# First attention without the scaling by the inverse row sum; the head norm takes epsilon times the squared sum

## The chip, the cores and the metric

The kernel runs on one core of one Trainium2 chip. The metric is the device time of one execution in microseconds (us), as a median over runs. Engines are named as the profile names them: PE (TensorE, matmuls), PEld (its weight loads), DVE (VectorE), ACT (ScalarE), POOL (GpSimd) and SP (SyncE, which issues most transfers). "L1688" is line 1688 of the kernel before.

## The reference

The kernel computes a two-layer encoder over 1024 tokens of width 1024 in float32. Layer 0 is a differential attention, layer 1 a latent attention, and a squared-ReLU MLP follows each. Only the attention of layer 0 is touched. It has 8 heads; each head has two score maps, and for a block of 128 queries:

```python
s = einsum(q, k) * scale + rel_bias            # two components c = 0, 1
p = softmax(masked s)                          # each component by itself
a = p[:, :, 0] - lam * p[:, :, 1]
o = a @ v                                      # 128 values for one query
o = o * rsqrt(mean(o * o) + 1e-6) * w * (1 - lam_init)
```

With e1 and e2 the exponentials and l1 and l2 their row sums, a = e1/l1 - lam * e2/l2. That is (e1 - lam * (l1/l2) * e2) / l1. The division by l1 is one factor for each query, and the norm that follows takes it out again, except for the epsilon in it.

## The kernel before, in words

A head is worked off in eight steps, s = 0 to 7, one for each block of 128 queries; step s has (s+1)*128 keys. All engines run the same order of steps, written out by hand (`heads0`, one for each engine), and meet at semaphores. Two query blocks make a pair, and the output and its norm are computed by pairs (256 queries).

For one block s the work goes round the engines so:

- PE computes both score maps (`scores0`, L1682), one step ahead: in step s it issues those of block s+1.
- DVE adds the bias, takes the maximum and writes the sum to `prob(s)` (`max0`, L1157), and writes the negated maxima (L1161).
- ACT takes both exponentials with their row sums l1, l2 in `st[:, 6:8]` (`exps0`, L712).
- DVE takes the reciprocals of both sums (L1210), the factor -lam*l1/l2 (L1212), and then e1 plus factor times e2 over the whole width (L1214), which raises `a_raw`.
- ACT multiplies the result by 1/l1 in place (`scale0`, L718) and raises `a_ready`.
- In step s+1 PE waits for `a_ready` and transposes the block in 128x128 pieces into PSUM tile TB (`turn0`, L1585), in one or two groups of up to four; ACT and DVE take it out of TB as a high and a low part (L696, L1137), and DVE raises `t_evac`. TB is a single bank, so a group waits until the one before is taken out.
- When both blocks of a pair are there, PE multiplies them with V (`values0`, L1666) into VB: in step 2 for pair 0, in 4 for pair 1, in 6 for pair 2, and in step 0 of the next head for pair 3.

The norm of a pair follows one step later, in steps 3, 5 and 7, and in step 1 of the next head for pair 3. ACT squares VB (`out_square`, L740), PE sums the squares over the partitions with a product by `ones` (`square_sum`, L1688), ACT takes the logarithm with scale and epsilon and then exp(-0.5 x) (`rms_of_pair`, L727 and L730), and DVE multiplies (`norm_out`, L1190). In ACT's order `scale0` of the step stands between `out_square` and `rms_of_pair`. After `rms_of_pair` ACT rounds a slab of weights for the next head (`split_hi`, L650) in steps 0, 1 and 3, and DVE computes its low part (`split_lo`, L1055).

PE has more in its order: the projections of the next head, in twelve half pieces of 12 products (`proj0`, L1578, `HALF_PIECES`). There is one after the transposes of a block in every step but step 0, and a second one after `square_sum` or the scores in steps 1, 2, 3, 5 and 7 as listed. ACT and DVE take the finished pieces out (`copy_piece0`, L690; `lo_piece0`, L1176, both between the exponentials and the second group of transposes of a block). The last head has no projections. DVE also does 8 multiply-adds of another product in each head (`ada_mac`, L1069); PE sums their result with 4 products that stream one column each (`mod_block`, L1599).

Of the kernel before, what the change touches and what calls it, by code (L numbers as in the profile page):

```python
# [18 lines left out]
ALU = mybir.AluOpType  # L19
ACT = mybir.ActivationFunctionType  # L20

P = 128
# [5 lines left out]
NQ = S // P  # L28
# [4 lines left out]
HD = 64  # L33
# [6 lines left out]
LN_EPS, RMS_EPS = 1e-5, 1e-6  # L40
# [7 lines left out]
PAIR = 2 * P  # L48
# [71 lines left out]
def encoder(nc, x, c, pos_offset, ada_w, ada_b, ln_g, ln_b, rel_table, w_qkv, w_o0, lq1, lk1, lq2,  # L120
# [3 lines left out]
    with ctx:  # L124
        def sb(name, shape, dt=F32):
            return ctx.enter_context(nc.sbuf_tensor(name, shape, dt))
# [18 lines left out]
        ones = sb("ones", [P, P])  # L145
# [4 lines left out]
        aff = sb("aff", [P, 7, KT])  # L150
        st = sb("st", [P, 18])
        soft = sb("soft", [P, 4 + 2 * NQ])
        posi = sb("posi", [P, 1], I32)
        lam = sb("lam", [P, 4 + REL_BUCKETS])

        ident = cst[:, 0:P]
# [14 lines left out]
        def prob(s): return X[:, 2 * (s % 2), :], X[:, 2 * (s % 2) + 1, :]  # L171
        bias = [X[:, 4, :], X[:, 5, :]]
        vT = X[:, 6, :]
        osq, oraw, orstd, ofin = (X[:, 7, i * PAIR:(i + 1) * PAIR] for i in range(4))
# [21 lines left out]
        VB = ps("VB", HALF)  # L196
# [8 lines left out]
        eps_ln, eps_rms = st[:, 11:12], st[:, 12:13]  # L205
# [437 lines left out]
        def _(act):  # L643
# [68 lines left out]
                    nc.scalar.activation(w, w, ACT.Exp, bias=st[:, 4 + comp:5 + comp],  # L712
                                         accum_out=st[:, 6 + comp:7 + comp]).then_inc(a0["p_ready"], 1)

            def scale0(h, s):
                act.wait_ge(a0["a_raw"], NQ * h + s + 1)
                w = prob(s)[0][:, 0:(s + 1) * P]
                nc.scalar.activation(w, w, ACT.Copy, scale=st[:, 8:9]).then_inc(a0["a_ready"], 1)  # L718

            def a_hi(h, s, part):  # L720
                dst, nb = at_group(0, s, part, AT0)
                copy_t(a0, 14 * h + group_of0(s, part), dst, t_psum(nb))
# [1 line left out]
            def rms_of_pair(h, pair):  # L724

                act.wait_ge(a0["ms_ready"], 4 * h + pair + 1)
                nc.scalar.activation(orstd, VB[:, PAIR:2 * PAIR], ACT.Ln, scale=1.0 / (2 * HD), bias=eps_rms)\  # L727
                    .then_inc(act_seq, 1)
                act.wait_ge(act_seq, 4 * h + pair + 1)
                nc.scalar.activation(orstd, orstd, ACT.Exp, scale=-0.5).then_inc(a0["r_ready"], 1)  # L730
# [11 lines left out]
            def heads0(h0, i, last=False):  # L742
                h, p = h0 + 2 * i, h0 % 2
                proj = not (last and h0 % 2)
                g0 = G_QKV + 3 * (h0 + 1)
                for s in range(NQ):
                    square = (h, (s - 3) // 2) if s in (3, 5, 7) else (h - 1, 3) if s == 1 and not is_first(h) else None
                    store = {0: None if is_first(h) else (h - 1, 2), 2: None if is_first(h) else (h - 1, 3),
                             4: (h, 0), 6: (h, 1)}.get(s)
                    if s >= 1:  # L750
                        a_hi(h, s - 1, 0)
                    elif not is_first(h):
                        a_hi(h - 1, NQ - 1, 0)
                    exps0(h, s)
                    if s == 0 and not is_first(h):
                        copy_piece0(p, h, LAST_PIECE)
                    if proj and s in PIECE_DONE:
                        copy_piece0(1 - p, h + 1, PIECE_DONE[s])
                    if s == 1:
                        for part in range(2):  # L760
                            copy_t(a0, 14 * h + 1 + part, V0[:, 0, 4 * part:4 * part + 4, :], t_psum(4))
                    if s - 1 >= 4:
                        a_hi(h, s - 1, 1)
                    elif s == 0 and not is_first(h):
                        a_hi(h - 1, NQ - 1, 1)
                    if store is not None:
                        out_hi(a0, store[0], store[1], P, ofin)
                    if square is not None:
                        out_square(*square)
                    scale0(h, s)  # L770
                    if square is not None:
                        rms_of_pair(*square)
                    if s == 0 and not proj:
                        split_hi(G_WO0, 0, KT, a0["pj_ready"], 6 * HEADS0)
                    if proj and s == 0:
                        split_hi(g0, 3 * i, KT, a0["pj_ready"], 6 * h + 4)
                    if proj and s == 1:
                        split_hi(g0 + 1, 3 * i, KT, a0["pj_ready"], 6 * h + 6)
                    if proj and s == 3:
                        split_hi(g0 + 2, 3 * i, KT, a0["pj_ready"], 6 * h + 8)  # L780
# [267 lines left out]
        def _(dve):  # L1048
# [144 lines left out]
            def heads0(h0, i, last=False):  # L1193
                h, p = h0 + 2 * i, h0 % 2
                proj = not (last and h0 % 2)
                g0 = G_QKV + 3 * (h0 + 1)
                own.body(h, 2 * NQ)
                dve.wait_ge(bias_masked, h + 1)
                for s in range(NQ):
                    norm = (h, (s - 3) // 2) if s in (3, 5, 7) else (h - 1, 3) if s == 1 and not is_first(h) else None  # L1200
                    store = {0: None if is_first(h) else (h - 1, 2), 2: None if is_first(h) else (h - 1, 3),
                             4: (h, 0), 6: (h, 1)}.get(s)
                    max0(h, p, s)
                    if s >= 1:
                        a_lo(h, s - 1, 0)
                    elif not is_first(h):
                        a_lo(h - 1, NQ - 1, 0)
                    n = (s + 1) * P
                    dve.wait_ge(a0["p_ready"], 2 * (NQ * h + s + 1))
                    own(nc.vector.reciprocal(st[:, 8:10], st[:, 6:8]))  # L1210

                    own(nc.vector.scalar_tensor_tensor(st[:, 10:11], st[:, 6:7], lam[:, 3:4], st[:, 9:10],  # L1212
                                                       ALU.mult, ALU.mult))
                    nc.vector.scalar_tensor_tensor(prob(s)[0][:, 0:n], prob(s)[1][:, 0:n], st[:, 10:11],  # L1214
                                                   prob(s)[0][:, 0:n], ALU.mult, ALU.add).then_inc(a0["a_raw"], 1)
                    if s == 0 and not is_first(h):
                        lo_piece0(p, h, LAST_PIECE)
                    if proj and s in PIECE_DONE and PIECE_DONE[s] // 2 != 1:
                        lo_piece0(1 - p, h + 1, PIECE_DONE[s])
                    if s == 1:  # L1220
                        for part in range(2):
                            blocks = slice(4 * part, 4 * part + 4)
                            lo_t(a0, 14 * h + 1 + part, V0[:, 1, blocks, :], TB[:, :].rearrange("p (b q) -> p b q", q=P),
                                 V0[:, 0, blocks, :])
                    if s - 1 >= 4:
                        a_lo(h, s - 1, 1)
                    elif s == 0 and not is_first(h):
                        a_lo(h - 1, NQ - 1, 1)
                    for t in MACS.get(s, ()):
                        ada_mac(4 + h, t)  # L1230
                    if s == 2 and not is_first(h):
                        mod_add(3 + h, block_cols(0, 3 + h))
                    if store is not None:
                        out_lo(a0, store[0], store[1], P, ofin)
                    if norm is not None:
                        norm_out(*norm)
                    if s == 0 and not proj:
                        split_lo(G_WO0, 0, KT)
                    if proj and s == 0:
                        split_lo(g0, 3 * i, KT)  # L1240
                    if proj and s == 1:
                        split_lo(g0 + 1, 3 * i, KT)
                    if proj and s == 3:
                        split_lo(g0 + 2, 3 * i, KT)
                own.end_body()
# [325 lines left out]
        def _(pe):  # L1571
# [70 lines left out]
            def turn0(h, s, part):  # L1642

                ix = group_of0(s, part)
                if part == 0:
                    pe.wait_ge(a0["a_ready"], NQ * h + s + 1)
                pe.wait_ge(a0["t_evac"], 14 * h + ix)
                for b in range(4 * part, min(s + 1, 4 * part + 4)):
                    ins = transpose_to(TB[:, (b % 4) * P:(b % 4 + 1) * P], prob(s)[0][:, b * P:(b + 1) * P])
                ins.then_inc(a0["t_ready"], 1)  # L1650
# [34 lines left out]

            def square_sum(h, pair):
                pe.wait_ge(a0["o_sq"], 4 * h + pair + 1)
                mm(VB[:, PAIR:2 * PAIR], ones[:, :], osq, start=True, stop=True).then_inc(a0["ms_ready"], 1)  # L1688

            def heads0(h0, i, last=False):  # L1690
                h, p = h0 + 2 * i, h0 % 2
# [314 lines left out]
```

## Time and profile before

| | before |
|---|---|
| median of 3 runs | 3235.27 us (3229.88 to 3240.05) |
| the profiled execution | 3228.4 us |
| its span | 3226.7 us |
| mean granted PE clock | 0.937 |
| PE busy | 2729.6 us (85%) |
| PEld busy | 2239.3 us (69%) |
| DVE busy | 1639.5 us (51%) |
| ACT busy | 1131.9 us (35%) |

The busy times are unions over the whole span. The attention of layer 0 is only the part from about 150 to 745 us of it. The chain that ended last is not of use here: it ends in the output's transfers. What the change touches is read from the waits and from the order of time in that part.

### The profile page before, as it was taken

To read this page: it belongs to the slowest core of one execution; us is meant where nothing else is said; L and a number is where in the kernel's file an instruction comes from. 1 tells how busy PE (TensorE), PEld (TensorE's weight loads), DVE (VectorE), ACT (ScalarE), POOL (GpSimd) and SP (SyncE) were. 2 spreads that over 40 slices of the span, in tenths; PEclk is the share of its full clock that TensorE was granted. 3 is DMA by queue.
4 is the path that set the end of the run, shared out by engine and by line. 5 is a ranking of instruction groups with operands and counts; after the bars stand their busy time and mean duration, and the time that the engine had idled before them with its cause. 6 is when DMAs were issued, how large, how long until landed. Compare 5 with 4: busy or idle time off the path is not lost. (4 is left out here: it accounts for less than half of the span.)

```text
span 3226.7 us, 38108 instructions
## 1 busy us (share of the span) xinstructions
PE 2729.6 (85%) x12732; PEld 2239.3 (69%) x12732; DVE 1639.5 (51%) x2833; ACT 1131.9 (35%) x2070; POOL 301.1 (9%) x314
## 2 busy tenths in 40 slices
PE   1688878868599999999939788888785999999995
PEld 1567767657378888888727677777564888888883
DVE  3466666662544343434482777777436323232325
ACT  0355555551341221213043556666305212130312
POOL 2000000000000000000361222222000000000000
PEclk9999999978799999999969999999897999999997
DMA  6322222233014132322212111111510111111111
GB/s 200 128 62 66 76 66 72 67 145 114 20 52 118 58 98 72 89 87 62 81 48 52 22 31 27 31 26 41 181 46 20 52 46 51 46 46 52 46 39 52
DMA packets 268778, 216.65 MB, mean 67 GB/s; under 512 B 36967, under 2 KB 244118, under 8 KB 268702
## 3 DMA queue, kind: packets, MB, share of 16 engines
q1 hardware_dynamic: 251662, 156.98, 16.4%
q0 software_dynamic: 17040, 58.73, 5.9%
q8 instruction: 38, 0.62, 0.1%
q14 instruction: 38, 0.31, 0.0%
HBM read 186.28 MB, written 33.59 MB: 68 GB/s over the span
## 5 line engine op out<-in xcount | busy, mean ns | idle before, releaser
L1578 PE MATMUL PA<-U,W 128*128 128x512 f32 x3840 | 945.7, 402 | 126.8 <-DVE W L1055 44.0
L1578 PEld LDWEIGHTS PA<-U,W 128*128 128x128 f32 x3840 | 731.4, 193 | 289.7 <-issue 89.7
L1578 PE MATMUL SC<-U,W 128*128 128x512 f32 x2064 | 482.1, 393 | 27.4 <-DVE U L1380 23.6
L650 ACT ACTIVATE W<-raw 128x1024 fp32r<-128x1024 f32 (+1 forms) x207 | 201.9, 975 | 773.3 <-PE PA L1578 357.4
L1578 PEld LDWEIGHTS SC<-U,W 128*128 128x128 f32 x2064 | 391.1, 190 | 112.0 <-issue 25.8
L1578 PE MATMUL PA<-H,W 128*128 128x512 f32 x1536 | 355.1, 391 | 0.0
L1578 PE MATMUL SC<-H,W 128*128 128x512 f32 x1536 | 353.4, 390 | 0.0
L1578 PEld LDWEIGHTS SC<-H,W 128*128 128x128 f32 x1536 | 288.4, 188 | 59.7
L1578 PEld LDWEIGHTS PA<-H,W 128*128 128x128 f32 x1536 | 287.6, 188 | 59.5
L1055 DVE TENSOR_TENSOR W<-raw,W 128x1024 fp32r<-128x1024 f32 (+1 forms) x207 | 245.5, 1186 | 116.5 <-ACT W L650 115.5
L1303 DVE SCALAR_TENSOR_TENSOR X<-PA,aff,X 128x512 f32 (+1 forms) x80 | 59.9, 751 | 285.1 <-PE PA L1578 268.9
L1303 DVE SCALAR_TENSOR_TENSOR X<-SC,aff,X 128x512 f32 (+1 forms) x80 | 60.0, 751 | 275.4 <-PE SC L1578 257.6
L505 POOL DMA_DIRECT2D ada<-in_ada_w x96 | 68.8, 717 | 1294.2 <-DVE acc L1069 1098.3
L1137 DVE TENSOR_TENSOR H<-TB,H 128x512 fp32r<-128x512 f32 (+3 forms) x216 | 122.6, 568 | 113.4 <-ACT H L696 112.9
L696 ACT ACTIVATE H<-TB 128x512 fp32r<-128x512 f32 (+3 forms) x216 | 107.7, 499 | 202.8 <-PE TB L1585 201.4
L1585 PE MATMUL TB<-cst,X 128*128 128x128 f32 (+1 forms) x712 | 122.7, 288 | 47.9 <-DVE H L1137 31.4
L1666 PE MATMUL VB<-H 128*128 128x256 f32 (+1 forms) x480 | 90.0, 363 | 69.9 <-DVE H L1137 69.7
L1879 PE MATMUL SC<-H 104*128 104x512 f32 (+3 forms) x576 | 140.0, 371 | 0.0
L1395 DVE SCALAR_TENSOR_TENSOR tmp<-PA,tmp 128x512 f32<-128x512 f32 x64 | 44.3, 692 | 187.5 <-ACT tmp L876 187.5
L1666 PEld LDWEIGHTS VB<-H 128*128 128x128 f32 x480 | 87.8, 277 | 74.5 <-DVE H L1137 39.9
L1395 DVE SCALAR_TENSOR_TENSOR tmp<-SC,tmp 128x512 f32<-128x512 f32 x64 | 44.3, 692 | 186.6 <-ACT tmp L876 186.6
L1069 DVE SCALAR_TENSOR_TENSOR acc<-ada,cact,acc 128x512 f32<-128x512 f32 x168 | 126.0, 750 | 24.2 <-DMA ada<-in_ada_w 20.0
(206 smaller groups left out, 3037.4 us busy)
## 6 DMA issues: line engine op xcount, KB each, us to landing
raw<-in_ffn_w SPq DMA_DIRECT2D x128, 512.0 KB, 4.1
ada<-in_ada_w POOLq DMA_DIRECT2D x96, 512.0 KB, 4.8
U<-attention_out SPq DMA_DIRECT2D x4, 3584.0 KB, 17.5
raw<-in_da_w_qkv SPq DMA_DIRECT2D x24, 512.0 KB, 4.2
attention_out<-ostage SPq DMA_DIRECT2D x32, 256.0 KB, 2.8
X<-residual SPq DMA_DIRECT2D x2, 4096.0 KB, 15.6
attention_out<-ostage SPq DMA_DIRECT2D x64, 128.0 KB, 2.3
X<-in_x SPq DMA_DIRECT2D x2, 2048.0 KB, 8.5
```

The lines of the kernel that those rows point to most:

```text
L505: pool.dma_start(ada[:, u % 2, :, :], src[:, 2 * u:2 * u + 2, bass.ds(b * BW, BW)]).then_inc(ada_in[u % 2], 16)
L650: nc.scalar.activation(W[:, slot, 0, 0:kt * P], raw[:, slot, 0:kt * P], ACT.Copy).then_inc(w_hi, 1)
L696: nc.scalar.activation(hi_dst, src, ACT.Copy).then_inc(s["t_hi"], 1)
L1055: nc.vector.tensor_tensor(W[:, slot, 1, 0:kt * P], raw[:, slot, 0:kt * P], W[:, slot, 0, 0:kt * P].bitcast(F32), ALU.subtract).then_inc(w_ ...
L1069: ins = nc.vector.scalar_tensor_tensor(acc[:, :], src, by, acc[:, :], ALU.mult, ALU.add)
L1137: nc.vector.tensor_tensor(dst, src, hi_ap.bitcast(F32), ALU.subtract).then_inc(s["t_evac"], 1)
L1303: nc.vector.scalar_tensor_tensor(tile, dense_bank[2 * ((g + k) % 2) + hf], by, tile, ALU.mult, ALU.add).then_inc(d_evac, 1)
L1395: nc.vector.scalar_tensor_tensor(tmp[:, 2 + hf, :], dense_bank[2 * ((g + k) % 2) + hf], 0.0, tmp[:, hf, :], ALU.max, ALU.mult).then_inc(d_ ...
L1578: ins = mm(bank, W[:, slot, a, kt * P:(kt + 1) * P], moving(b, kt)[:, cols], start=kt == first and (a, b) == SPLIT[0], stop=kt == last and ...
L1585: return nc.tensor.transpose(out_ap, in_ap, ident[r0:r0 + n, r0:r0 + n])
L1666: ins = mm(VB[:, c0:PAIR], V0[:, a, j, :], AT0[:, b, j, c0:PAIR], start=j == 0 and (a, b) == SPLIT[0], stop=j == last and (a, b) == SPLIT[-1])
L1879: ins = mm(SC[s % 2][:, k], q1(p, a)[0:MR.stop, s * P:(s + 1) * P], k1(p, b)[0:MR.stop, k], start=(a, b) == SPLIT[0], stop=(a, b) == SPLIT ...
```

## The change

The scaling by 1/l1 on ACT (`scale0`) is dropped, 64 times. PE's transposes wait for `a_raw` of DVE directly. The output of a pair is then l1 times what it was, so its mean square is l1*l1 times as large, and epsilon has to be multiplied by l1*l1 for the norm to be the same. DVE computes 128 * 1e-6 * l1 * l1 for the block, one value for each partition, and writes it to a column of the new tile `eps_l`. PE adds these values to the sum of squares in PSUM: for each block of the pair one product of the column, repeated over 128 columns as the stationary operand, with the identity as the moving one (128 columns, float32). The logarithm on ACT has no bias any more. The reciprocal on DVE is taken of one column in place of two.

```diff
+        eps_l = sb("eps_l", [P, NQ])
...
-            def scale0(h, s):
-                act.wait_ge(a0["a_raw"], NQ * h + s + 1)
-                w = prob(s)[0][:, 0:(s + 1) * P]
-                nc.scalar.activation(w, w, ACT.Copy, scale=st[:, 8:9]).then_inc(a0["a_ready"], 1)
...
-                nc.scalar.activation(orstd, VB[:, PAIR:2 * PAIR], ACT.Ln, scale=1.0 / (2 * HD), bias=eps_rms)\
+                nc.scalar.activation(orstd, VB[:, PAIR:2 * PAIR], ACT.Ln, scale=1.0 / (2 * HD))\
                     .then_inc(act_seq, 1)
...
                         out_square(*square)
-                    scale0(h, s)
                     if square is not None:
                         rms_of_pair(*square)
...
                     dve.wait_ge(a0["p_ready"], 2 * (NQ * h + s + 1))
-                    own(nc.vector.reciprocal(st[:, 8:10], st[:, 6:8]))
+                    nc.vector.scalar_tensor_tensor(eps_l[:, s:s + 1], st[:, 6:7], 2 * HD * RMS_EPS, st[:, 6:7],
+                                                   ALU.mult, ALU.mult).then_inc(a0["l_inv"], 1)
+                    own(nc.vector.reciprocal(st[:, 9:10], st[:, 7:8]))
...
                 if part == 0:
-                    pe.wait_ge(a0["a_ready"], NQ * h + s + 1)
+                    pe.wait_ge(a0["a_raw"], NQ * h + s + 1)
...
             def square_sum(h, pair):
                 pe.wait_ge(a0["o_sq"], 4 * h + pair + 1)
-                mm(VB[:, PAIR:2 * PAIR], ones[:, :], osq, start=True, stop=True).then_inc(a0["ms_ready"], 1)
+                mm(VB[:, PAIR:2 * PAIR], ones[:, :], osq, start=True, stop=False)
+                pe.wait_ge(a0["l_inv"], NQ * h + 2 * pair + 2)
+                for k in range(2):
+                    ins = mm(VB[:, PAIR + k * P:PAIR + (k + 1) * P],
+                             eps_l[:, 2 * pair + k:2 * pair + k + 1].to_broadcast([P, P]), ident, start=False, stop=k == 1)
+                ins.then_inc(a0["ms_ready"], 1)
```

## Rows read from the trace of the kernel before

**Rows 1.** Busy time by engine over the first attention (us, instructions, granted clock).

```profile
150.00:745.00 595.00, 472.05 (x2336) 397.82 (x2337) 390.31 (x993) 321.43 (x676) 26.36 (x42) 0.89 0.25 77
```

**Rows 2.** PE's waits, 150 to 745 us: total us, times, longest.

```profile
PE VB L1666 <- DVE H L1137: 69.7, 16, 5.4
PE VB L1688 <- ACT X L740: 19.6, 23, 1.6
...
PE TB L1585 <- ACT X L718: 6.3, 12, 1.4
```

**Rows 3.** Groups by line, 160 to 745 us: busy us, mean ns, idle before.

```profile
L718 ACT ACTIVATE X<-X,st 128x256 f32<-128x256 f32 (+7 forms) x63 | 49.0, 777 | 16.3 <-DVE X L1214 16.2
...
L1212 DVE SCALAR_TENSOR_TENSOR st<-st,lam 128x1 f32<-128x1 f32 x62 | 13.6, 219 | 2.2
```

**Rows 4.** PE in order of time, head 4, steps 1 to 7: start, duration, idle.

```profile
465.74 0.70 PE L1688 MATMUL VB<-X,ones 128*128 128x256 f32 x2 [0.96 <-ACT X L740]
...
472.93 0.94 PE L1599 MATMUL VB<-ones,acc 128*128 128x1 f32 x8
...
481.63 0.65 PE L1688 MATMUL VB<-X,ones 128*128 128x256 f32 x2
...
489.43 1.52 PE L1666 MATMUL VB<-H 128*128 128x256 f32 x12
491.22 0.66 PE L1585 MATMUL TB<-cst,X 128*128 128x128 f32 x4 [0.27 <-ACT X L718]
...
497.01 0.70 PE L1688 MATMUL VB<-X,ones 128*128 128x256 f32 x2 [0.66 <-ACT X L740]
...
509.92 3.86 PE L1666 MATMUL VB<-H 128*128 128x256 f32 x18 [4.22 <-DVE H L1137]
...
513.99 3.00 PE L1578 MATMUL PA<-U,W 128*128 128x512 f32 x12
...
518.59 0.70 PE L1688 MATMUL VB<-X,ones 128*128 128x256 f32 x2 [0.85 <-ACT X L740]
518.94 3.12 PE L1578 MATMUL PA<-U,W 128*128 128x512 f32 x12
```

**Rows 5.** ACT in order of time, the same head, steps 3 and 5.

```profile
482.31 0.47 ACT L727 ACTIVATE X<-VB,st 128x256 f32<-128x256 f32 x1 [0.51 <-PE VB L1688]
...
483.14 1.05 ACT L650 ACTIVATE W<-raw 128x1024 fp32r<-128x1024 f32 x1
...
497.58 0.94 ACT L718 ACTIVATE X<-X,st 128x768 f32<-128x768 f32 x1 [0.62 <-DVE X L1214]
498.43 0.46 ACT L727 ACTIVATE X<-VB,st 128x256 f32<-128x256 f32 x1
```

**Rows 6.** DVE in order of time, the same head, steps 3 to 6.

```profile
484.22 1.23 DVE L1055 TENSOR_TENSOR W<-raw,W 128x1024 fp32r<-128x1024 f32 x1
...
486.99 0.17 DVE L1161 TENSOR_SCALAR st<-st 128x2 f32<-128x2 f32 x1
487.09 0.69 DVE L1137 TENSOR_TENSOR H<-TB,H 128x512 fp32r<-128x512 f32 x1
...
499.37 0.48 DVE L1190 SCALAR_TENSOR_TENSOR X<-VB,aff,X 128x256 f32<-128x256 f32 x1 [0.17 <-ACT X L730]
...
506.61 2.79 DVE L1176 SCALAR_TENSOR_TENSOR H<-PA,H 64x512 fp32r<-64x512 f32 x4 [0.69 <-ACT H L690]
```

**Rows 7.** PE's waits for L718 in the first head and the last.

```profile
153.39 0.47 PE L1585 MATMUL TB<-cst,X 128*128 128x128 f32 x1 [1.39 <-ACT X L718]
155.60 4.38 PE L1578 MATMUL PA<-U,W 128*128 128x512 f32 x12 [1.73 <-DVE W L1055]
...
735.15 1.11 PE L1585 MATMUL TB<-cst,X 128*128 128x128 f32 x4 [1.09 <-ACT X L718]
```

**Rows 8.** Windows around the values product of pair 3 (columns as Rows 1).

```profile
529.80:534.00 4.20, 4.20 (x19) 4.20 (x20) 2.27 (x9) 0.00 (x0) 0.00 (x0) 0.50 0.48 143
534.10:537.00 2.90, 2.90 (x18) 2.46 (x17) 1.06 (x4) 1.25 (x5) 0.00 (x0) 1.00 0.17 51
```

**Rows 9.** PE in order of time: that product in heads 4, 5 and 6.

```profile
529.79 4.92 PE L1666 MATMUL VB<-H 128*128 128x256 f32 x24 [5.22 <-DVE H L1137]
...
605.17 4.76 PE L1666 MATMUL VB<-H 128*128 128x256 f32 x24 [5.31 <-DVE H L1137]
...
680.38 4.71 PE L1666 MATMUL VB<-H 128*128 128x256 f32 x24 [5.31 <-DVE H L1137]
```

## The prediction

> **What bounds the kernel now.** The change touches only the first attention, so I read that stretch and not the whole span. First the busy times by engine [rows 1]: PE works 472 of 595 us, DVE 390, ACT 321. PE is the nearest to full, but 123 us of it are idle, so no engine is the bound alone. Then who ends PE's waits [rows 2]: the largest group, 69.7 us, is the values product that waits for DVE's low part; 19.6 us are `square_sum` waiting for ACT's squares; only 6.3 us, in 12 waits, end with the scaling L718 that the change drops. Then ACT's own groups [rows 3]: the scaling is 49.0 us of busy time, but ACT has time to spare, so its busy time is not a gain by itself. Last the order of time in one full head [rows 4 to 6], where the path through a head can be followed.
>
> That path, for head 4: in step 1 PE waits 0.96 us for the squares, does `square_sum` at 465.74, and then works without a gap to `square_sum` of step 3 at 481.63. From there it goes by ACT: L727 starts at 482.31 after 0.51 us of waiting for PE, then the second activation, then the slab's high part at 483.14 (1.05 us), and DVE's low part starts at 484.22, just when that ends [rows 5, 6]. Steps 4 to 6 run on DVE and ACT (maxima, exponentials, differences), with PE slack of 4.22 us in front of the values product at 509.92 [rows 4]. In step 6 DVE itself waits 0.69 us for ACT's copies before L1176 [rows 6]. From 509.92 PE carries it again, through `square_sum` of step 7 at 518.59 and 12 products behind it, to the last transposes and the product at 529.79 [rows 4, 9].
>
> **Part 1: the scaling on ACT goes.** 64 instructions, about 49 us of ACT [rows 3]. On the path it stands only where a wait on it isn't covered. In step 4 PE waits 0.27 us for it at 491.22 [rows 4], but PE has 4.22 us of slack two steps later: nothing. In step 5 it holds L727 until 498.43, after the square sum of 497.01 with its 0.70 us has ended at 497.71 [rows 4, 5]; 0.7 us could go, but there the new products take its place (part 2), and DVE's L1190 at 499.37 had waited only 0.17 us [rows 6]. In the first head PE waits 1.39 us for it at 153.39, but next it waits 1.73 us for a weight slab that ACT rounds behind that short scaling [rows 7]; the bounds are 0 and 1.4, I take 0.4. In the last head PE waits 1.09 us at 735.15; the longer square sum ends some 0.35 us earlier than the scaling did, so 0.35 remains. Together -0.75 us. The upper bound of the gain is all that PE waited for it, 6.3 us [rows 2].
>
> **Part 2: two small products for each pair.** 32 pairs, 64 products. The trace has no such product; the nearest row is `square_sum` itself, which streams 256 float32 columns as two instructions, and the new ones stream 2 x 128, as four. Its occupancy: the 12 projection products behind it show 3.12 us where they otherwise show 3.00 and start 0.35 us after it [rows 4], so 0.35 + 0.12 = 0.47 us. From below: the 8 instructions of `mod_block`, full weight loads with one column each, show 0.94 us together, so four are 0.47 us, or 0.4 if the last one's latency is taken off [rows 4]. From above: the whole 0.70 us of the square sum, latency included. I take 0.48 us. The added wait for `l_inv` is for a value written at least one step earlier, so only the instruction counts; behind it stand PE's projections, and ACT's L727 waits for the result.
>
> The Trainium skill ("TensorE: Matmul & The Clock Gate", section Back-to-back issue gap) puts a sustained stream of weight load and product at about 81 ns for 128 columns. Four instructions would be 0.32 us by that, and 22 times it 7.1 us in place of 10.6; the page doesn't say it for float32, and no row here is that short, so the rows decide.
>
> Where does it lie on the path? Step 1: yes, PE is the path behind it. Step 3: yes, by ACT's L727, the slab's high part and DVE's L1055, +0.48. Step 5: L727 may start at 497.71 + 0.48 + some 0.05 = 498.24 and did start at 498.43; DVE is ready for L1190 at 499.2 anyway: nothing. Step 7: yes, PE again. So three for each of the six heads 1 to 6 (18), two in head 0, and in head 7 the one of step 1 and the closing one: 22 x 0.48 = +10.6 us. The other ten are covered by DVE and ACT. Bounds: 22 x 0.40 = 8.8 and 22 x 0.70 = 15.4.
>
> **Part 3: one small operation on DVE for each block.** 64 instructions on one column. A full one of this kind is 0.219 us [rows 3], but nothing waits for it and the next instruction may start before it ends: L1161, 0.17 us long, is followed 0.10 us after its start [rows 6]. So 0.10 to 0.22 us, I take 0.12. DVE carries the path in step 4 (in step 3 the slab on ACT covers it, in step 6 and step 0 the waits for ACT's copies, elsewhere PE): 8 heads x 0.12 = +1.0 us. Were it on the path in all four steps 3 to 6, it would be 32 x 0.22 = 7 us. The reciprocal of one column in place of two: nothing.
>
> Sum of the work: 10.6 + 1.0 - 0.75 = +10.8 us.
>
> **Part 4: PE's clock.** After each of the two long waits in a head the values product runs at the lower level: the window from 529.80 to 534.00 was granted 0.50 (1.2 GHz), the next one 1.00 (2.4 GHz) [rows 8]. That product has 24 instructions in 4.92 us, and 18 in 3.86 us after the 4.22 us wait, while 12 at the full clock take 1.52 us [rows 4, 9]: 0.127 us each, so 3.05 and 2.28 us, and the two low stretches cost 1.87 + 1.58 = 3.45 us for each head. The product of pair 3 starts at 529.79, 605.17 and 680.38, 75.38 and 75.21 us apart, and gets shorter each time, 4.92, 4.76, 4.71 us [rows 9]: the later it comes, the less of it falls into the low stretch. A head that is made 1.5 us longer therefore gets part of it back, at half a us for each us of delay at each of the two products, as long as the clock still comes back after so short a stretch of work. Bounds: nothing given back, or nearly all (6 heads x 1.5 us = 9 us). Since a delay adds up over the heads and must at some point run past the end of the low stretch, where a new one begins, I take a bit under half of that, -4 us.
>
> Forecast: +10.8 - 4 = +6.8 us. The profiled execution would go from 3228.4 to 3235.2 us; it lay 6.9 us below the median of the runs, and I add the sum to the median: 3235.3 + 6.8 = **3242 us**. What this kernel's measurement can tell from no change is about 0.3%, 9.7 us.
>
> **Rivals.**
> 1. *The path takes the full sum, and the clock gives nothing back or takes more.* Price: 22 products of 0.48 to 0.70, 1 to 4 us for DVE and no gift: +10 to +18 us, 3246 to 3253. It decides where, after a wait that ends later, the work before the expected return is too little to lift the clock, and the product then runs low to its end. For it: in the first heads no row shows a short low stretch. Against it: the falling durations [rows 9]. This is the case on the other side, slower by more than 0.3%.
> 2. *Heads lock to the clock.* The starts 75.38 and 75.21 us apart may be going towards a fixed distance, with each head's delay wholly given back until the 3.45 us are used up. Then only the first head's delay and the last's stay: +1 to +3 us, 3237 us.
> 3. *The freed ACT shortens the waits for the low part too.* The 69.7 us of waits [rows 2] end with L1137, behind ACT's copies. If ACT were late there because of the scaling, 6.3 us and a tenth of 69.7 us could go, -13 us against +10.8 and -4 of clock: 3229 us, and less with cheap products. Against it: ACT does the exponentials, the four copies and the high part in one go in those steps, and waits for PE before them; the scaling comes behind.
>
> **How the numbers follow.** Forecast case (sum with part given back, +3.5 to +9.7) 0.50; rival 1, 0.27; rival 2, 0.16; rival 3, 0.07. Faster by over 0.3% needs rival 3 or a cheaper product than any row: 0.06. Slower by over 0.3% is rival 1: 0.28. Within: 0.66. The range leaves out about one in ten on each side: from 3232 (rival 2 and the spread of about 5 us of the runs) to 3252 (rival 1 with the products at 0.60 us).
>
> **What would show it.** The four new instructions end some 0.5 us after those of `square_sum`; L727 no longer has L718 before it and waits for PE in all steps; the wait of DVE's L1055 behind step 3 moves with it; PE's waits that end with L1214 are next to none; the values wait of step 6 stays near 4.2 us and that of step 0 near 5.2. Heads 1 to 6 last 76.8 us each if nothing is given back, near 75.3 us under rival 2, and in between by the forecast. The forecast is wrong if the new products take under 0.3 or over 0.7 us, or if the 4.22 and 5.22 us waits change by more than 0.5 us.

## The result, and the profile after

| | before | after |
|---|---|---|
| median | 3236.5 us (6 runs, 3229.9 to 3240.1) | 3248.1 us (6 runs, 3246.1 to 3249.5) |
| profiled execution, its span | 3228.4, 3226.7 us | 3246.1, 3244.4 us |
| mean granted PE clock | 0.937 | 0.930 |
| the first attention, from its first scores to its first output projection | 144.92 to 749.87 = 604.95 us | 145.68 to 771.62 = 625.94 us |
| the rest of the span behind it | 2476.8 us | 2472.8 us |

The ratio is 1.0039, with a 95% interval from 1.0026 to 1.0052: slower by 11.6 us, where 6.8 us had been forecast. The time lies in the range of 3232 to 3252 us. The profiled executions differ by more, 17.7 us, and all of that is in the first attention, which grew by 21.0 us. Execution times of the kernel before spread over 25 us in the later measurements (24 runs, 3227.8 to 3253.0), so a term is read below from intervals inside the traces, not from one difference of two spans.

PE in order of time after the change, one full head from step 0 to step 7 (start, duration, engine, line, tiles, idle before and who ended it). L1685 is the old square sum, L1688 the new products:

```profile
544.81 5.03 PE L1663 MATMUL VB<-H 128*128 128x256 f32 x24 [5.22 <-DVE H L1132]
...
554.60 0.65 PE L1582 MATMUL TB<-cst,X 128*128 128x128 f32 x4 [0.71 <-DVE H L1132]
556.21 0.70 PE L1685 MATMUL VB<-X,ones 128*128 128x256 f32 x2 [0.96 <-ACT X L736]
556.75 0.61 PE L1688 MATMUL VB<-cst,eps_l 128*128 128x128 f32 x4
557.11 3.02 PE L1575 MATMUL PA<-U,W 128*128 128x512 f32 x12
...
572.54 0.65 PE L1685 MATMUL VB<-X,ones 128*128 128x256 f32 x2
573.02 0.61 PE L1688 MATMUL VB<-cst,eps_l 128*128 128x128 f32 x4
...
588.34 0.70 PE L1685 MATMUL VB<-X,ones 128*128 128x256 f32 x2 [1.11 <-ACT X L736]
...
601.23 4.10 PE L1663 MATMUL VB<-H 128*128 128x256 f32 x18 [3.75 <-DVE H L1132]
...
611.13 0.70 PE L1685 MATMUL VB<-X,ones 128*128 128x256 f32 x2 [0.86 <-ACT X L736]
```

Beside [rows 4]: the two products are four instructions, and the projections behind them start 0.90 us after the square sum in step 1 (557.11 - 556.21), 0.35 us before. As the 12 projections then show 3.02 us and not 3.12, the products occupy 0.55 - 0.10 = 0.45 us. ACT and DVE in step 3 show the path that the prediction took there. The logarithm is L723, the slab's high part L651, its low part L1050; L1205 is the new operation on DVE, L1207 the reciprocal:

```profile
573.66 0.38 ACT L723 ACTIVATE X<-VB 128x256 f32<-128x256 f32 x1 [1.57 <-PE VB L1688]
574.08 0.42 ACT L726 ACTIVATE X<-X 128x256 f32<-128x256 f32 x1
574.40 1.05 ACT L651 ACTIVATE W<-raw 128x1024 fp32r<-128x1024 f32 x1
```

```profile
570.63 0.16 DVE L1205 SCALAR_TENSOR_TENSOR eps_l<-st 128x1 f32<-128x1 f32 x1 [0.85 <-ACT X L713]
570.71 0.16 DVE L1207 RECIPROCAL st<-st 128x1 f32<-128x1 f32 x1
...
575.48 1.23 DVE L1050 TENSOR_TENSOR W<-raw,W 128x1024 fp32r<-128x1024 f32 x1 [0.33 <-ACT W L651]
```

The logarithm waits 1.57 us for PE (0.51 before, with the scaling ahead of it) [rows 5], and DVE now waits 0.33 us for ACT's slab. Its low part starts 2.94 us after the square sum (575.48 - 572.54), 2.59 us before (484.22 - 481.63) [rows 4, 6], so 0.35 us later. The new operation on DVE starts the reciprocal 0.08 us later.

In PE's waits from 150 to 765 us (total us, times, longest), the wait for the scaling is gone. The values product waited 69.7 us before and the square sum 19.6 us [rows 2], so the others changed by some 3 us each:

```profile
PE VB L1663 <- DVE H L1132: 66.4, 16, 5.4
PE VB L1685 <- ACT X L736: 22.7, 23, 1.6
...
PE TB L1582 <- DVE X L1211: 1.9, 2, 1.0
```

What the prediction did not have is in another head, also in step 1. First PE in order of time, then a window (us, busy PE, PEld, DVE, ACT, POOL, granted clock, DMA share, GB/s):

```profile
315.33 0.66 PE L1582 MATMUL TB<-cst,X 128*128 128x128 f32 x4 [0.70 <-DVE H L1132]
316.95 1.05 PE L1685 MATMUL VB<-X,ones 128*128 128x256 f32 x2 [0.96 <-ACT X L736]
317.79 1.06 PE L1688 MATMUL VB<-cst,eps_l 128*128 128x128 f32 x4
318.51 3.97 PE L1575 MATMUL PA<-U,W 128*128 128x512 f32 x12
```

```profile
317.30:320.50 3.20, 3.20 (x11) 2.66 (x10) 0.53 (x2) 1.58 (x3) 0.00 (x0) 0.50 0.00 0
```

The clock was 1.00 from 316.00 to 317.00 and 0.50 (1.2 GHz) from 317.30 to 320.30. So it fell in the middle of step 1, just after the square sum had started, behind PE's waits of 0.70 and 0.96 us with four transposes between them. The projections take 3.97 us in place of 3.02. No full head of the profiled execution before has that: its six stretches from step 1 to step 3 all show 1.00. The table shows where the time went, as intervals between square sums of neighbouring norms in heads 1 to 6 (from one start to the next, in us):

| interval | before | after |
|---|---|---|
| step 1 to 3 | 15.85 to 15.89 | 16.33 in two heads, 17.92 to 17.97 in four |
| step 3 to 5 | 15.38 to 15.39 | 15.79 to 15.81 |
| step 5 to 7 | 21.49 to 21.65 | 21.58 to 21.68 in three heads, 22.34 to 22.84 in three |
| step 7 to 1 of the next head | 22.32 to 22.75, and 25.38 at the loop's end | 23.05 to 23.37, and 26.21 at the loop's end |

("The loop's end" is where the loop over pairs of heads jumps back, between heads 3 and 4. The last row starts in heads 0 to 5.) From step 7 to step 7, heads take 77.97 to 78.82 us after (82.27 over the loop's end), 75.11 to 75.30 before (75.63 for the first, 78.23 over the loop's end). Work at an unchanged clock, as the experiments below show, accounts for +0.46, +0.43, nothing and +0.47 us in the four rows. In the first row the granted clock is 1.00 in the short intervals and 0.90 or 0.91 in the four long ones; in the third it is 0.92 in the short ones and 0.85 in the long ones, as in these two of the kernel after:

```profile
270.88:293.72 22.84, 18.15 (x85) 15.56 (x85) 16.38 (x37) 10.19 (x20) 1.57 (x3) 0.85 0.18 52
350.69:372.32 21.63, 17.03 (x85) 14.46 (x85) 16.32 (x37) 10.19 (x20) 1.86 (x3) 0.92 0.18 57
```

So +1.6 us in four heads and +0.8 to 1.3 us in three heads go with a lower clock. The last row has 0.85 on both sides, and the 0.1 to 0.4 us a head that it grew beyond the work aren't explained by that mean.

### The profile page after: what moved, and what is told of

Same layout as the page of the kernel before. It is cut to its first block and busy times, and to the rows that moved or that the text cites. A ratio compares the mean times of both kernels' runs of the same rounds, so it can differ in the third digit from the quotient of the medians.

```text
span 3244.4 us, 38364 instructions
## 1 busy us (share of the span) xinstructions
PE 2754.9 (85%) x12860; PEld 2265.5 (70%) x12860; DVE 1643.0 (51%) x2897; ACT 1085.8 (33%) x2006; POOL 303.0 (9%) x314
## 5 line engine op out<-in xcount | busy, mean ns | idle before, releaser
L651 ACT ACTIVATE W<-raw 128x1024 fp32r<-128x1024 f32 (+1 forms) x207 | 201.9, 975 | 770.1 <-PE PA L1575 357.1
L1050 DVE TENSOR_TENSOR W<-raw,W 128x1024 fp32r<-128x1024 f32 (+1 forms) x207 | 245.4, 1186 | 116.8 <-ACT W L651 116.0
```

The costliest lines, as they stand in the source:

```text
L651: nc.scalar.activation(W[:, slot, 0, 0:kt * P], raw[:, slot, 0:kt * P], ACT.Copy).then_inc(w_hi, 1)
L1050: nc.vector.tensor_tensor(W[:, slot, 1, 0:kt * P], raw[:, slot, 0:kt * P], W[:, slot, 0, 0:kt * P].bitcast(F32), ALU.subtract).then_inc(w_ ...
```

## The experiments

e1 to e4, e5 to e8 and e9 to e11 were measured on three different chips. The kernel before was measured again beside each: 3237.6 us (24 runs), 3236.9 us (9) and 3239.0 us (13). A difference of a few us between experiments of different groups is therefore weaker evidence than the intervals inside the traces.

### e1 and e2: one half of the change each

```diff
# e1: the kernel before, plus
+            nc.vector.memset(eps_l[:, :], 2 * HD * RMS_EPS)      # once
-    ... ACT.Ln, scale=1.0 / (2 * HD), bias=eps_rms)
+    ... ACT.Ln, scale=1.0 / (2 * HD))
-    mm(VB[:, PAIR:2 * PAIR], ones[:, :], osq, start=True, stop=True)
+    mm(VB[:, PAIR:2 * PAIR], ones[:, :], osq, start=True, stop=False)
+    ... the two products with eps_l
# e2: the changed kernel, minus the two products
```

> The kernel before, scaling on ACT kept, with only the two small products for each pair added (from a constant column 128*1e-6, the logarithm without bias; the same result). Theory A (the products on the path, three a head, and a clock that falls more often): most of the change, +9 to +14 us over before, heads 1 to 6 longer by 2 to 3.5 us each, of which about 1.2 to 1.5 us is work. Theory B (DVE's extra operation and the order of the freed ACT matter, the products are covered): under +4 us.

> The changed kernel without the two small products, so the norm leaves out epsilon (a factor below what its output shows); DVE still computes the column. Theory A: back to the time before or a little below it, -4 to +1 us against before, since the scaling was hardly on the path. Theory B: stays at +8 us or more. If the scaling had been on the path as PE's waits for it say at most, -6 us.

e1: 3247.6 us (12 runs, 3238.8 to 3252.8), against 3237.6 us for the kernel before on the same chip (24 runs), ratio 1.0019 (1.0000 to 1.0039). The medians are 10 us apart, the ratio's interval is wide because of the spread of the kernel before. In its trace the interval from step 3 to 5 is 15.74 us and heads last 78.0 to 78.8 us (82.3 over the loop's end): the products alone make what the whole change makes. e2: 3235.7 us (12 runs, 3233.3 to 3239.1), ratio 0.9988 (0.9970 to 1.0006): no difference shown; step 3 to 5 is 15.38 us again. Its norm leaves out epsilon. Theory A holds in what it says of the work, and theory B falls: the freed ACT and the operation on DVE are next to nothing.

e2 showed more. Without any products, its heads 1 to 3 last 78.4 to 78.5 us and heads 5 and 6 last 75.1 and 75.3 us, in one execution of the same instructions. Step 1 of head 1 and of head 5, PE in order of time:

```profile
237.74 0.63 PE L1582 MATMUL TB<-cst,X 128*128 128x128 f32 x4 [0.81 <-DVE H L1132]
239.33 0.89 PE L1685 MATMUL VB<-X,ones 128*128 128x256 f32 x2 [0.96 <-ACT X L736]
239.68 4.71 PE L1575 MATMUL PA<-U,W 128*128 128x512 f32 x12
...
548.88 0.66 PE L1582 MATMUL TB<-cst,X 128*128 128x128 f32 x4 [0.71 <-DVE H L1132]
550.50 0.70 PE L1685 MATMUL VB<-X,ones 128*128 128x256 f32 x2 [0.96 <-ACT X L736]
550.85 3.12 PE L1575 MATMUL PA<-U,W 128*128 128x512 f32 x12
```

```profile
239.70:243.10 3.40, 3.40 (x10) 2.64 (x9) 1.54 (x3) 1.75 (x3) 0.00 (x0) 0.50 0.02 5
...
550.50:553.90 3.40, 3.40 (x15) 2.79 (x16) 1.73 (x3) 1.75 (x3) 0.00 (x0) 1.00 0.00 0
```

Nearly the same waits (0.81 and 0.96 us, 0.71 and 0.96 us), and 4.71 against 3.12 us. So a head of this code has two lengths, some 3.3 us apart: 1.6 us of it from step 1 to 3 (clock 0.90 against 1.00), 1.2 us from step 5 to 7 (0.85 against 0.92) and some 0.4 us from step 7 to 1. The long heads are there without the products, so the products as such don't make them. The kernel before was profiled only in one of its fastest executions; its slower ones (up to 3253 us) may have had long heads too, but no trace shows it.

### e3 and e4: both kernels with the two long waits filled

```diff
 def values0(h, pair):
     pe.wait_ge(a0["o_fin"], 4 * h + pair)
+    for k in range({2: 24, 3: 32}.get(pair, 0)):
+        mm(VB[:, PAIR:2 * PAIR], V0[:, 0, 0, :], V0[:, 0, 0:2, :], start=True, stop=True)
```

> The kernel before, with products whose result nobody reads put into PE's two long waits of a head (24 and 32 products of 256 columns, V with V, into the half of VB that is free), to keep the clock at its upper level. Theory A: the low stretches at the values products of pairs 2 and 3 go, 3.4 us a head, 20 to 27 us less than before; if the filling runs past the wait, up to 1 us a head less gain. Theory C (the level of the clock in these products is not on the path): no gain, or slower by the filling.

> The changed kernel with the same filling. Theory A: with the clock held up in both, the difference from the filled kernel before is the work alone, 22 products of 0.48 us and 1 us on DVE less 0.75: +8 to +12 us, 1.5 to 1.7 us a head. If the difference is that of the unfilled pair in head length (3.3 us a head), the clock is not the cause of the excess, and the work is twice what I took.

e3: 3206.6 us (6 runs, 3204.8 to 3208.6), ratio to before 0.9896 (0.9867 to 0.9925), 31 us less. e4: 3217.3 us (7 runs, 3216.9 to 3218.5), ratio 0.9931 (0.9906 to 0.9956). Theory C falls. The gain of e3 is above the 20 to 27 us that I had expected. Between the profiled executions it is 21.4 us (3228.4 to 3207.0); in the medians it is more because the kernel before has many executions that are longer than its profiled one, while e3's lie within 4 us. In e3 heads 1 to 6 last 71.9 to 72.0 us (75.1 over the loop's end); the values products show 2.34 us for 18 and 3.07 us for 24 where they were 3.86 and 4.92 [rows 4, 9]:

```profile
494.14 3.12 PE L1663 MATMUL VB<-H 128*128 128x256 f32 x24
498.61 2.34 PE L1668 MATMUL VB<-H 128*128 128x256 f32 x18 [1.35 <-DVE H L1137]
...
511.49 4.08 PE L1663 MATMUL VB<-H 128*128 128x256 f32 x32
516.96 3.07 PE L1668 MATMUL VB<-H 128*128 128x256 f32 x24 [1.40 <-DVE H L1137]
```

The difference of e4 from e3, 10.7 us, is inside what I had expected of the work, but partly for a wrong reason: in four of e4's six heads step 1 to 3 still takes 17.9 us, 1.6 us too long, at a clock of 0.90. By these intervals some 6.4 us of the difference are the clock and not work.

### e5: the waits of step 1 filled too

```diff
# e4, plus
 def turn_v0(h, part):
     pe.wait_ge(a0["v_evac"], 2 * h + part + 1)
+    if part == 1 and not is_first(h):
+        for k in range(3):
+            mm(PA[1][:, 0:P], ones[:, :], ident, start=True, stop=True)
 def square_sum(h, pair):
+    if pair == 3:
+        for k in range(4):
+            mm(PA[1][:, 0:P], ones[:, :], ident, start=True, stop=True)
```

> The filled changed kernel, with small unread products also in PE's two waits of step 1 (three before the second group of V's transposes, four before the square sum of pair 3). Theory D (an extra low stretch of the clock in step 1, which comes or not by where the head lies against the clock's changes, is the rest of the difference): step 1 to step 3 takes 16.3 us in all heads instead of 17.9 in four of six, some 5 to 6 us less than the filled changed kernel, about 3211 us. Theory E (what makes the interval 17.9 us is a wait for another engine): it stays at 17.9, and the filling adds to it.

3211.5 us (5 runs, 3210.5 to 3212.8), 5.8 us less than e4, and 16.31 to 16.33 us from step 1 to 3 in all six heads; heads last 73.26 to 73.29 us (75.87 over the loop's end). Theory D holds. PE in step 1, no idle time left in it:

```profile
527.23 0.83 PE L1653 MATMUL PA<-cst,ones 128*128 128x128 f32 x6
528.11 0.66 PE L1582 MATMUL TB<-cst,X 128*128 128x128 f32 x4
528.61 1.06 PE L1691 MATMUL PA<-cst,ones 128*128 128x128 f32 x8
529.73 0.70 PE L1693 MATMUL VB<-X,ones 128*128 128x256 f32 x2
530.27 0.61 PE L1696 MATMUL VB<-cst,eps_l 128*128 128x128 f32 x4
530.63 3.02 PE L1575 MATMUL PA<-U,W 128*128 128x512 f32 x12
```

### e6 and e7: which products are covered

```diff
# e6: e4 without the two products
# e7: e4 with them only where pair == 1 (step 5)
+    if pair != 1:
+        mm(VB[:, PAIR:2 * PAIR], ones[:, :], osq, start=True, stop=True).then_inc(a0["ms_ready"], 1)
+        return
```

> The filled changed kernel without the two small products, so the norm leaves out epsilon. If the scaling on ACT was off the path and DVE's extra operation too, each interval between square sums is that of the filled kernel before within 0.1 us, and the time 3205 to 3207 us unless the clock falls in step 1. If dropping the scaling helped anywhere, it is below 3204 us.

> The filled changed kernel with the two small products only for pair 1, whose norm is in step 5; for the other pairs the norm leaves out epsilon. By the prediction's step these are covered by DVE's multiply-adds: all intervals as without products, less than 1 us more than the kernel with none. If every product counts, +3 to +4 us (8 x 0.45).

e6: 3201.3 us (4 runs, 3196.2 to 3203.5); e7: 3201.1 us (4 runs, 3200.1 to 3203.9). The products of step 5 cost nothing that a time shows. In the traces the interval from step 5 to 7 is 19.89 us without them and 20.05 us with them (481.83 to 501.88), and 20.06 us in e3, which has the scaling. So dropping the scaling is worth 0.17 us a head there, and the products take it back. e6 lies below 3204 us, where I had expected it only if dropping the scaling helped. But 8 x 0.17 us is 1.4 us, and it is 5.3 us below e3. The profiles show 2.8 us of that in the first attention, although one of its intervals from step 1 to 3 is long (17.51 us; e7 has one of 17.44). The rest I can't place.

### e8 and e11: cheaper products

```diff
# e8: e4, e11: e5, each with
-    eps_l = sb("eps_l", [P, NQ])
+    eps_l = sb("eps_l", [P, NQ], F32R)
+    ident_r = sb("ident_r", [P, P], F32R)      # copied once from ident
-    eps_l[...].to_broadcast([P, P]), ident, ...
+    eps_l[...].to_broadcast([P, P]), ident_r[:, :], ...
```

> The filled changed kernel with the small products in the rounded float32 format (half the instructions, one pass). They should take about half, 0.2 us in place of 0.43: intervals 1 to 3, 3 to 5 and 7 to 1 each 0.2 us shorter, 22 x 0.2 = 4 to 5 us less than the filled changed kernel, or up to 9 if the clock stays up in step 1 as well. If a product's cost is the wait in front of it and not its columns, no change.

> The changed kernel with all fillings and the small products in the rounded format: the cheapest whole version so far. By the sum of the parts 0.2 us less for each of three intervals in a head than with float32 products (3211.5 us), 4 to 5 us: 3206 to 3208 us, level with the filled kernel before, so that the change as such is worth nothing even then. If freeing ACT is worth the 0.17 us a head that the kernel without products showed in step 5 to 7, 3205 us.

e8: 3209.4 us (5 runs, 3206.3 to 3216.9), 7.9 us less than e4. That is more than the 4 to 5 us of the products: only two of its six intervals from step 1 to 3 are long (17.66 and 17.71 us, the others 16.07 to 16.11), where e4 has four. Two instructions in place of four, and the projections follow 0.71 us after the square sum in place of 0.90:

```profile
505.39 0.70 PE L1695 MATMUL VB<-X,ones 128*128 128x256 f32 x2 [0.85 <-ACT X L737]
505.74 0.52 PE L1698 MATMUL VB<-ident_r,eps_l 128*128 128x128 f32 x2
506.10 2.98 PE L1577 MATMUL PA<-U,W 128*128 128x512 f32 x12
```

These rows are of e11, which gave 3204.9 us (4 runs, 3203.1 to 3209.5). Its intervals are 16.08, 15.54, 19.88 and 20.83 us; e5 has 16.32, 15.82, 20.05 and 21.07. So halving a product's instructions saves 0.24, 0.28 and 0.24 us where it is on the path, and 0.17 us from step 5 to 7, which is then as short as in e6, without products.

### e9 and e10: the fillings apart, and the control

```diff
# e9: the changed kernel with the filling of step 1 only
# e10: e3 with the filling of step 1 as well
```

> The changed kernel with the unread small products only in the two waits of step 1, the two long waits unfilled. Theory D: the clock stays up in step 1, the interval from step 1 to step 3 is 16.3 us in every head, 6 to 10 us less than the changed kernel, about 3239 us; the heads are then 1.3 us longer than before by work, and the long waits keep their low stretches, in a place that may differ. Theory E (a step's wait for another engine): no gain.

> The filled kernel before with the filling of step 1 as well. Its clock didn't fall in step 1, so nothing is to be had there: the same as the filled kernel before within 2 us, 3205 to 3208 us, and 4 to 7 us less than the changed kernel filled in the same way. If the filling itself costs time on PE, it shows here, as an interval from step 1 to step 3 over 15.9 us or from 7 to 1 over 20.7 us.

e9: 3238.2 us (10 runs, 3235.5 to 3241.2), ratio to before 0.9995 (0.9982 to 1.0009). That is 9.9 us less than the changed kernel, by seven small products a head that nobody reads, and step 1 to 3 is 16.29 to 16.33 us in all six heads. In the medians the whole loss of the change is gone, although its products are all still there. In the traces it isn't gone: e9's heads last 76.8 to 78.3 us, its first attention 613.0 us, against 625.9 us for the changed kernel and 605.0 us for the kernel before in its fast profiled execution. The low stretches from step 5 to 7 stayed, and came out short or long (21.4 to 22.9 us). e10: 3205.1 us (4 runs, 3203.6 to 3206.1), 1.5 us less than e3, within what I expected, and 15.85 to 15.88 us from step 1 to 3: the filling costs PE nothing. e5 is 6.4 us above e10, both filled alike, inside the 4 to 7 us expected.

e10 and e11 (measured side by side), at 3205.1 and 3204.9 us, both beat the two kernels by over 31 us, and are level: with the cheapest products and the clock held, the change is worth nothing either way. Not tried were the small products issued inside PE's waits, ahead of the square sum. Whether they could be hidden there stays open.

## Why the prediction was right in its time, and where not

The time lies in the range partly by luck. The work was taken 4.4 us too high, the clock 9.2 us too low, and the two errors cancel in part. The 11.6 us lie outside the forecast's own case (+3.5 to +9.7) and in that of rival 1 (+10 to +18).

- *Part 1, the scaling leaves almost no gain*: right. e2 shows 15.38 us from step 3 to 5, as before, and e6 against e3 0.17 us a head from step 5 to 7. In the first head, from the first scores to the square sum of step 3, the change saves 0.31 us (176.77 - 144.92 = 31.85 before, 177.22 - 145.68 = 31.54 after), where 0.4 was taken: the weight slab is ready 1.3 us sooner, but the 12 products behind it take 5.36 us in place of 4.38. The term of the last head wasn't read apart. 49 us of ACT work bought 1 to 2 us.
- *Part 2, the price of two products*: 0.48 us was taken, 0.45 us is read from the rows. For the four intervals of a head e5 against e10 gives +0.46, +0.43, -0.01 and +0.47 us, the work of DVE included; e1, which has only the products, gives +0.36 for the second. Three of four are on the path, step 3 by way of ACT's slab, and step 5 is not (e7).
- *Part 3, DVE's operation*: over-sized. The start moves by 0.08 us, and e1 (without it, with the scaling) against the changed kernel is 15.74 against 15.80 us from step 3 to 5, 0.06 us for a head. 0.12 was taken. Alone, without the products, it shows nothing there (e2).
- *The sum of the work, +10.8 us*: the filled pair e5 against e10, with the clock at 1.00 in all full heads except over the loop's end (0.93), gives 6.4 us in the medians and 7.1 us in the first attention (587.2 against 580.1). The sum was too high in three places. The six full heads grew by 7.7 us against 9.4 predicted (1.35 us each against 1.56, and less over the loop's end). The first head got 0.2 us shorter against +0.7. The last head was taken at +0.7 too, and e5's is 0.4 us shorter from step 7 to step 7.
- *Part 4, the clock gives back 4 us*: this is the step that failed. What it predicted, "a head that is made 1.5 us longer therefore gets part of it back", isn't what happened: after the change the heads take 78.0 to 78.8 us, more than the 76.8 us without any gift. The clock took time instead: 1.6 us in step 1 of four heads, by a low stretch that the trace of before doesn't have, and 0.8 to 1.3 us in step 5 to 7 of three. In the medians I estimate that at 11.6 - 6.4 = +5.2 us, where -4 us was forecast; in the two profiled executions it is 21.0 - 7.1 = 13.9 us. The profiled one of before was among its fastest, all its full heads of the short length. A warning stood in its trace: the stretch from step 5 to 7 of head 0 (192.16 to 214.38) took 22.22 us at a clock of 0.85, where heads 1 to 6 took 21.49 to 21.65 us at 0.92.
- *Rival 1* (the full sum, and a clock that gives nothing back or takes more) is nearer to the truth than the forecast, in price and in kind. Its place, the work after a long wait, is a part of it (step 5 to 7); it didn't have step 1. *Rival 2*, heads locked to the clock, has a grain: heads do come at two lengths, near 75.2 and 78.5 us, but a longer head goes to the longer one in place of being given back its delay. Why the clock falls at step 1 in one alignment and not in the other isn't settled here; shown is that filling PE's waits there takes the fall away (e5, e9). *Rival 3* had nothing in it: the wait of step 0 is 5.22 us as before, and that of step 6 fell from 4.22 to 3.75 us because PE comes 0.45 us later.

## What to carry to other kernels

Taking 49 us of work off an engine that waits elsewhere bought 1 to 2 us, and 0.45 us on the engine that the path goes through came back three times in each head. Where an engine's clock depends on its waits, a small edit's price is its work plus what it does to the clock: compare the two versions with the waits filled, so that the work can be read alone. And the low stretches themselves were the larger matter: unread products in waits that were already there gave 31 us. A median over executions that differ in their low stretches can hide or feign a small effect (e9), so read it beside intervals of one trace.

## What the hardware showed that I had not expected

- PE's clock fell behind waits of only 0.70 and 0.96 us, with four transposes between them, and was 0.50 from 317.30 to 320.30 us; in other heads of the same execution the same sequence ran at 1.00.
- One code has two lengths of head, 78.4 to 78.5 and 75.1 to 75.3 us in one execution (e2).
- A float32 product of 128 columns is two instructions; in the rounded format it is one, and a pair of them occupies about half as much (0.24 to 0.28 us less of 0.45; e11 against e5).
